# Latent pages turned by transfers and VectorE in a hybrid decoder step

## What is computed

```python
def _decompress(c_kv, w_ukv, g_kn):
    kv = jnp.einsum('btc,chd->bthd', c_kv, w_ukv)
    return _rmsnorm(kv[..., :NOPE], g_kn), kv[..., NOPE:]

def _attn_partial(qn, qp, kn, kp, v, mask):
    s = (jnp.einsum('bqhd,bkhd->bhqk', qn, kn) + jnp.einsum('bqhr,bkr->bhqk', qp, kp)).astype(jnp.float32) * SCALE
    ...
    m = jnp.max(s, axis=-1)
    e = jnp.exp(s - m[..., None])
    return m, jnp.sum(e, axis=-1), jnp.einsum('bhqk,bkhd->bhqd', e, v.astype(jnp.float32))

def _sample_attention(qn, qp, kn_new, kp_new, v_new, cache_ckv, cache_kpe, layer, page_table, w_ukv, g_kn):
    def step(carry, phys):
        c_blk = cache_ckv[layer, phys]
        kp_blk = cache_kpe[layer, phys]
        kn_blk, v_blk = _decompress(c_blk, w_ukv, g_kn)
        return _merge(carry, _attn_partial(qn, qp, kn_blk, kp_blk, v_blk, None)), None
    carry, _ = lax.scan(step, init, page_table.T)
    ...
```

## Time and profile before

| what | value |
|---|---|
| median of 3 runs | 1372.71 us (1370.44 to 1373.48) |
| profiled execution, its own time | 1373.91 us |
| its span in the trace | 1372.0 us |
| TensorE busy | 1301.0 us (95%) |
| VectorE, ScalarE, GpSimd busy | 707.8, 459.9, 150.8 us |
| mean granted TensorE clock | 0.973 |

### The profile page before, as it was taken

How to read it: one execution, slowest core, us unless ns; L and a number is a source line. 1 busy time by engine, 2 the same in 40 slices (tenths; PEclk the granted TensorE clock), 3 DMA queues, 4 the chain that set the end, 5 groups by cost and what they waited for, 6 DMA issues and landing times. The chain is left out here.

```text
span 1372.0 us, 26075 instructions
## 1 busy us (share of the span) xinstructions
PE 1301.0 (95%) x9543; PEld 750.1 (55%) x9543; DVE 707.8 (52%) x1749; ACT 459.9 (34%) x1108; POOL 150.8 (11%) x182
## 2 busy tenths in 40 slices
PE   5999999699999999999989999999999999989898
PEld 3545677556666666555445445666544444445343
DVE  3001436644665656555737876667666666520321
ACT  3001343233343433332434433434344444310220
POOL 0000314400020201114402230000000000000000
PEclk9999999789999999999999999999999999998999
DMA  5422121101111111131141113221334221101000
GB/s 206 155 74 54 32 62 32 52 19 37 37 37 37 37 37 37 37 71 36 40 129 41 40 39 113 97 90 43 86 112 116 68 69 53 49 0 35 16 16 35
DMA packets 82995, 81.49 MB, mean 59 GB/s; under 512 B 18946, under 2 KB 76611, under 8 KB 82868
## 3 DMA queue, kind: packets, MB, share of 16 engines
q1 hardware_dynamic: 80452, 73.87, 18.1%
q10 hardware_dynamic: 2416, 5.96, 1.2%
HBM read 75.72 MB, written 4.07 MB: 58 GB/s over the span
## 5 line engine op out<-in xcount | busy, mean ns | idle before, releaser
L500 PE MATMUL PS<-wk,c_T 128*128 128x512 f32 x1024 | 500.8, 612 | 0.0
L627 DVE TENSOR_REDUCE ssq<-sq__69 128x8 f32<-128x512 f32 x256 | 175.4, 685 | 221.1 <-ACT sq__69 L554 218.7
L500 PEld LDWEIGHTS PS<-wk,c_T 128*128 128x128 f32 x1024 | 176.3, 192 | 163.0 <-issue 145.7
L554 ACT ACTIVATE sq__69<-PS 128x512 f32<-128x512 f32 x256 | 152.8, 597 | 320.5 <-PE PS L500 320.2
L455 PE MATMUL PS<-cst,c_ring 128*128 128x128 f32 x512 | 83.0, 287 | 24.7 <-DVE c_ring L663 10.1
L1470 PE MATMUL PS<-xnT,w_ring 128*128 128x276 f32 x416 | 104.7, 409 | 0.0
L455 PEld LDWEIGHTS PS<-cst,c_ring 128*128 128x128 f32 x512 | 60.4, 147 | 69.7 <-issue 45.0
L1304 PE MATMUL PS<-w_ring,xnT 128*128 128x424 f32 x256 | 95.3, 530 | 2.1 <-DMA w_ring<-in_w_in 2.1
L1470 PEld LDWEIGHTS PS<-xnT,w_ring 128*128 128x128 f32 x416 | 79.9, 195 | 21.9 <-issue 4.1
L1304 PEld LDWEIGHTS PS<-w_ring,xnT 128*128 128x128 f32 x256 | 48.5, 193 | 46.8 <-issue 44.3
L2655 PE MATMUL PS<-w_g,nT 128*128 128x512 f32 x128 | 56.0, 594 | 0.0
(11 more groups left out here) (534 smaller groups left out, 1873.3 us busy)
## 6 DMA issues: line engine op xcount, KB each, us to landing
c_ring<-in_cache_ckv SPq DMA_DIRECT2D x256, 128.0 KB, 2.8
w_ring<-in_w_in SPq DMA_DIRECT2D x4, 1696.0 KB, 14.4
w_ring<-in_w_in SPq DMA_DIRECT2D x9, 512.0 KB, 5.0
r_ring<-in_cache_kpe SPq DMA_DIRECT2D x256, 16.0 KB, 1.8
w_o<-in_w_out SPq DMA_DIRECT2D x8, 512.0 KB, 3.7
w_g<-in_w_ple_gate SPq DMA_DIRECT2D x8, 512.0 KB, 3.6
xn<-in_x_prompt SPq DMA_DIRECT2D x4, 512.0 KB, 7.0
w_ring<-in_w_in SPq DMA_DIRECT2D x2, 1024.0 KB, 5.8
```

The source lines that it names most:

```text
L500: mm = pe.matmul(PS[:, NORM[v % 2], :], c_T[:, u % 2, k, t * P:(t + 1) * P], wk[:, k], start=(k == 0), stop=(k == 1))
L554: nc.scalar.activation(sq_[:, v % 2, :], PS[:, NORM[v % 2], :], ACT.Square).then_inc(no_sb, 1)
L627: dve.tensor_reduce(ssq[:, u % 2, t * H:(t + 1) * H], sq_[:, v % 2, :].rearrange("p (h c) -> p h c", h=H), AX.X, ALU.add).then_inc(red_sb, 1)
```

## The change

The latents are no longer turned on TensorE. `latent_blocks(u)` has ScalarE's queue issue four transfers inside SBUF, each of which puts 64 columns of the four pages on 32 partitions (`c_blocks`, one buffer), in pieces of 64 numbers. VectorE's `turned_c(u, t)` then transposes blocks of 32x32 and writes a page of `c_T`, four instructions a step; `c_T` has one buffer instead of two. The rows of `c_T` thereby stand in another order, and `wk` is loaded in that order by eight transfers instead of being copied from `wukv`. `dots(u)` moves from the last slot to slot 1, beside `values`; `turn_r` moves from slot 2 to slot 0; the copy of `dots_s` moves from VectorE to ScalarE. `c_ring` has five slots, `r_ring` three. In the rows block the first weights are loaded before the second x tile, and several small steps of VectorE, ScalarE, GpSimd and TensorE change places. The blocks for chunks, sequences and latents become one, without the two barriers; the sequences get one more page slot and the last stretch one less. The causal mask of the attention is added by VectorE in PSUM. The output stage keeps its order with some tiles at other addresses.

```diff
-RING = 4
+RING = 5
+R_RING = 3
...
-SEQ_SLOTS = 23
+SEQ_SLOTS = 24
...
-        sc = place("sc", [P, P])
         ew_q = place("ew_q", [P, P])
         ew = place("ew", [P, GT * QH])
         ms = place("ms", [P, 4])
         ring_at = place.at
-        c_T = place("c_T", [P, 2, 2, GT * P])
+        c_ring = place("c_ring", [P, RING, GT, KVL + 1])
+        blocks_at = place.at
+        c_blocks = place("c_blocks", [P, GT, GT, KVL // 4])
+        c_T = place("c_T", [P, 2, GT * P])
+        rope_at = place.at
         r_T = place("r_T", [P, P])
-        r_ring = place("r_ring", [P, RING, GT * ROPE])
+        r_ring = place("r_ring", [P, R_RING, GT * ROPE])
         w_ring_at = t1_at + 4 * (NT * D + KD * TEXT)
-        assert place.at <= w_ring_at
-        pages_at = place.at = w_ring_at
-        c_ring = place("c_ring", [P, RING, GT, KVL + 1])
...
+        def latent_blocks(eng, u):
+            eng.wait_ge(c_in[u % RING], 16 * GT * (u // RING + 1))
+            if u >= 1:
+                eng.wait_ge(ct_sb, u * GT)
+            for g in range(4):
+                eng.dma_start(c_blocks[32 * g:32 * g + 32].rearrange("p x t c -> p (x t c)"),
+                              c_ring[:, slot_of[u], :, g * (KVL // 4):(g + 1) * (KVL // 4)]).then_inc(b_in, 16)
...
-            def turn_c(u, k):
-                if k == 0:
-                    pe.wait_ge(c_in[u % RING], 16 * GT * (u // RING + 1))
-                    if u == 1:
-                        pe.wait_ge(k1_sb, 1)
-                    if u >= 2:
-                        pe.wait_ge(rp_sb, u - 1)
-                else:
-                    pe.wait_ge(k0_sb, u + 1)
-                for t in range(GT):
-                    mm = pe.transpose(PS[:, TURN, t * P:(t + 1) * P], c_ring[:, u % RING, t, k * P:(k + 1) * P], ident)
-                mm.then_inc((k0_ps, k1_ps)[k], 1)
...
             def dots(u):
+                pe.wait_ge(ct_sb, u * GT + GT)
...
             def norms(u, t):
                 v = u * GT + t
-                if t == 0:
-                    pe.wait_ge(k1_sb, u + 1)
+                pe.wait_ge(ct_sb, v + 1)
...
-            pe.wait_ge(ring_ready, 1)
-            turn_c(0, 0)
-            turn_c(0, 1)
+            yield
+            yield
             for u, t in slots:
-                ahead = u + 1 < NSTEP
                 if t == 0:
-                    if ahead:
-                        turn_c(u + 1, 0)
+                    turn_r(u)
                     if u >= 2:
                         turn_weights(u - 2)
                 if t == 1:
-                    if ahead:
-                        turn_c(u + 1, 1)
+                    dots(u)
                     if u >= 2:
                         values(u - 2)
-                if t == 2:
-                    turn_r(u)
-                    if u >= 1:
-                        turn_scale(u - 1)
-                if t == 3:
-                    dots(u)
+                if t == 2 and u >= 1:
+                    turn_scale(u - 1)
                 norms(u, t)
                 yield
...
+            def dotted(u):
+                if u >= 1:
+                    act.wait_ge(eq_sb, u)
+                act.wait_ge(rp_ps, u + 1)
+                nc.scalar.copy(dots_s[:].rearrange("p x c -> p (x c)"), PS[:, TURN, P:3 * P]).then_inc(rp_sb, 1)
...
-            turned_c(0)
+            latent_blocks(act, 0)
+            yield
+            yield
             for u, t in slots:
-                ahead = u + 1 < NSTEP
                 if t == 0:
+                    turned_r(u)
                     if u >= 2:
                         turned_weights(u - 2)
                     if u >= 1:
                         roots(u - 1)
-                    square(u, t)
-                if t == 1:
-                    if ahead:
-                        turned_c(u + 1)
-                    square(u, t)
-                if t == 2:
-                    turned_r(u)
-                    square(u, t)
                 if t == 3:
                     if u >= 1:
                         weights(u - 1)
-                    square(u, t)
+                    dotted(u)
+                square(u, t)
+                if t == 1 and u + 1 < NSTEP:
+                    latent_blocks(act, u + 1)
                 yield
...
-            def turned_c(u):
-                dve.wait_ge(k0_ps, u + 1)
-                dve.tensor_copy(c_T[:, u % 2, 0, :], PS[:, TURN, :]).then_inc(k0_sb, 1)
-
-            def dotted(u):
-                dve.wait_ge(rp_ps, u + 1)
-                dve.tensor_copy(dots_s[:].rearrange("p x c -> p (x c)"), PS[:, TURN, P:3 * P]).then_inc(rp_sb, 1)
+            def turned_c(u, t):
+                dve.wait_ge(b_in, 16 * 4 * (u + 1))
+                if u >= 1:
+                    dve.wait_ge(rp_ps, u)
+                    dve.wait_ge(no_ps, (u - 1) * GT + t + 1)
+                dve.transpose(c_T[:].rearrange("p k (t a x) -> p t x k a", t=GT, x=GT)[:, t],
+                              c_blocks[:, :, t, :].rearrange("p x (k c) -> p x k c", k=2)).then_inc(ct_sb, 1)
...
+            yield
+            for t in range(GT):
+                turned_c(0, t)
             dve.memset(c_ring[:, :, :, KVL:KVL + 1], 1.0).then_inc(ring_ready, 1)
-            turned_c(0)
+            yield
             for u, t in slots:
                 ahead = u + 1 < NSTEP
                 if t == 0:
-                    if ahead:
-                        turned_c(u + 1)
                     if u >= 1:
+                        turned_c(u, 3)
                         scales(u - 1)
                 if t == 1 and u >= 2:
                     merge(u - 2)
-                if t == 2 and u >= 1:
-                    score(u - 1)
-                if t == 3:
-                    dotted(u)
+                if t == 2:
+                    if u >= 1:
+                        score(u - 1)
+                    if ahead:
+                        turned_c(u + 1, 0)
+                if t == 3 and ahead:
+                    turned_c(u + 1, 1)
+                    turned_c(u + 1, 2)
                 reduce(u, t)
                 yield
...
-        on_sp = Stream(pages_sp(), lambda slot: min(NSTEP, max(RING, (slot - 2) // GT + RING - 1)))
+        on_sp = Stream(pages_sp(), lambda slot: min(NSTEP, slot // GT + 3))
...
+                tile_in(0)
                 weights(0)
+                for i in range(1, NT - 1):
+                    tile_in(i)
...
+        def seqs_sp(sp):
+            sp.wait_ge(l_ps, NP)
+            sp.wait_ge(rows_kept, 1)
...
+        def seqs_pe(pe):
+            on_pe.go(1)
+            pe.wait_ge(rows_kept, 1)
+            pe.wait_ge(wkv_sb, 1)
+            pe.wait_ge(half_sb, NP)
...
-        recycle()
         place = Region(nc, shifted_at, t1_at)
...
+                pe.wait_ge(so_sb, BS)
...
+            @block.tensor
+            def _(pe):
+                chunk_pe(pe)
+                seqs_pe(pe)
+                lat_pe(pe)
...
-                    pe.matmul(bank(u % 2)[:, 0:w], qT[:, h, i * P:(i + 1) * P], k_T[:, h, 0:w], start=True, stop=False)
-                    pe.matmul(bank(u % 2)[:, w - P:w], ident, con("causal"), start=False, stop=True).then_inc(sc_ps, 1)
+                    pe.matmul(bank(u % 2)[:, 0:w], qT[:, h, i * P:(i + 1) * P], k_T[:, h, 0:w], start=True, stop=True
+                              ).then_inc(sc_ps, 1)
...
                     dve.wait_ge(sc_ps, u + 1)
+                    V(dve.tensor_tensor(bank(u % 2)[:, w - P:w], bank(u % 2)[:, w - P:w], con("causal"), ALU.add))
```

1657 lines of the change are left out of this document (838 added, 819 removed).

## The result

The changed kernel takes **1602.57 us** (median of 4 runs, 1597.86 to 1613.4), the kernel before 1372.12 beside it: a ratio of 1.169 (95% interval 1.163 to 1.175). The forecast was 1364, its range ended at 1420. The sign was left open; the size is far out. The profiled execution took 1602.05 us, its span is 1600.2.

A forecast was written before the change was run, and what follows sets the result against it. TensorE's queue was taken to bound the kernel. The last stretch at +40 us and the rest at -49 gave -9, from the profiled 1373.9 to 1365, less 1.2 to the median: 1364 us; own range 1335 to 1390, full range 1300 to 1420.

The forecast's parts named there:

- its stations: Last stretch: first issue to first turn 4.9 us, first turn to dot products 2.9, dot products to next issue 3.55.
- Landing: Four transfers in a row: last issued after 1.95 us, lands 2.8 later, page loads add 0.15; 4.9 us.
- The upper bound of 6.6: Landing of the four transfers if their 512 KB move at half the state load's 239 GB/s.
- Rival 2: Small pieces at half rate: landing 6.6 us, step 13.2, last stretch 297, total 1400 us; chance 0.17.
- rival 3: Clock falls to 1.2 GHz in every step: step 14.5 us, last stretch 326, total 1426 us; chance 0.10.
- The turn: VectorE's 128x256 transpose, four a step: 0.41 us each, taken from a copy of as many elements.
- The other stages: All outside the last stretch: -49 us, among it chunks -14, sequences -4, latents -4, attention -10.
- Attention: Attention stage: -8.5 us for turns, -12 for masking matmuls, against VectorE's additions and waits; -10 taken (-18 to +3).
- start and rows: Start and RWKV rows: -2.5 us for earlier first weights, -6 for the first page turn's shorter wait; -8.5.
- the first barrier: Before the sequences: TensorE's 4.6 us idle and 1.5 of slow clock go; -6 us.
- the wait on wukv: Before the latents: the barrier's 5.8 us idle becomes a wait on the wukv weights' load; -2.5 us.
- Rival 1: Transfers hidden, TensorE bounds everywhere: last stretch 199 us, total 1299 us; chance 0.12.

The follow-up runs named there:

- the early issue: The changed kernel with ScalarE's four transfers issued one slot earlier, behind square (u,0) instead of (u,1): 1355.7 us, again 1362.94 us (ratio 0.992).
- the best version: The early issue plus two block buffers from page group 26, one transfer issued a slot, contiguous turns, mask back on TensorE: 1319.27 us, ratio 0.959.

## Why the prediction was wrong

The bound before, the loop and its stations were right: one buffer, the issue behind square (u,1), the first turn waiting, TensorE idle before the first norms. The terms of the sum were not. (The stations of the loop, 4.9, 2.9 and 3.55, add up to 11.35 and not 11.45, and the bounds to a range of 1332 to 1397 and not 1335 to 1390; neither slip matters here.)

- **Landing, 4.9 forecast, 8.0 measured.** The step that failed is "the last is issued after 3 x 0.65 = 1.95 and lands 2.8 later", with page loads at 0.15. Alone the four take 6.4: the first lands after 3.2 us and not 2.8, and the others follow at the 1.0 us that each takes on the engines and not at the 0.65 of their issue. Page loads and rope keys cost the other 1.6, since both kinds start at slot (u,1). The upper bound of 6.6 had the half rate, and was right for it; it lacked the contention.
- **Rival 2 and rival 3 were no alternatives.** I gave the half rate 0.17 and the lower clock 0.10 and priced each alone. A long landing makes the pause longer, the pause takes the clock down, and the slower matmuls stand in the loop. With the pause filled the stations are 7.7, 3.2 and 3.6 against my 4.9, 2.9 and 3.55: 2.8 for the landing and 0.3 for slower turns. The lower clock adds 1.1 us between turn and dot products, 0.75 behind them and 0.3 in the landing: 11.35 + 2.8 + 0.3 + 2.15 is 16.6, the measured median. My own two prices added would have been 13.2 + 3 = 16.2. That it comes near is luck: the 13.2 had no contention in it, and the 3 slowed more work than the clock did.
- **The turn, 0.41 forecast, 0.63 measured.** The row I took was right for the elements; the stride of the output, plain in the diff, was left out. Four a step are 0.9 us of VectorE; with the stride gone, 0.5 of it went out of the way from first turn to dot products (3.2 to 2.7 us at full clock).
- **The other stages, -49 forecast, +83 measured** (the table without its last stretch). The failed step is "the loop of 11.5 is shorter than their step of 15.6". The loop isn't a fixed length to be held against a step: it runs through the stage's own work too, and only what stands between issue and first turn can hide the landing. That is one slot on VectorE, about 4 us (3.7 in the median of the chunks; the forecast had 4.2 and was right in this). But the landing is 8.3 there and not 4.9, so VectorE doesn't stand 0.8 us, as I had it: it stands 73.4 us in 16 steps of the chunks, 46.0 in 15 and 25.4 in 7 of the next two stages, and its evictions for the stage stand behind it. And I priced such a stand at about a third of its length, where the chunks, 50 us above their forecast in 17 steps, lost 2.9 us a step to 4.1 us of standing. With the issue a slot earlier VectorE stands 0.3 us a step there and the chunks come to -12, near the forecast of -14. Sequences and latents come to -6 in one profile and to -1 in the other, against -10.5. For the chunks the terms were right as long as the landing is hidden; for the latents that isn't shown.
- **Attention, -10 forecast, +42 measured, +4 with the early issue.** The landing first: VectorE stands for the blocks, the maximum of the scores stands behind it, and TensorE waits for the exponential 34.7 us in seven stands. Then the mask: I wrote that VectorE and TensorE alternate and still counted the matmuls as mostly a gain. With the early issue ScalarE still waits 77.9 us of the attention for VectorE's maximum (64.2 before).
- **Right in size:** start and rows (-12.6 for -8.5), the first barrier (about 5 us for my 6), the wait on wukv in place of the second. Of the turns' 1.0 us of TensorE a step, 0.7 came: in the best version the step is 9.1 us in the median against 9.85 before.
- Rival 1, the hidden transfers, was priced at 1299 and given 0.12. With them hidden it is 1339 with the parts as they were, 1319 with turns and mask mended. I named its condition, the issue a slot earlier, without asking what that slot was worth: 240 us.

## What to carry to other kernels

Where a transfer replaces work and has one buffer, write down the queue of each engine from the issue to the first use: only that stretch hides the landing, whatever the length of a step. Price issue, landing, contention and clock as one chain, for they feed each other; if two of your rivals share a cause, add their prices. And before dropping a slow change, move its issue up a slot: that is one line.

## What the hardware showed

- Transfers from SBUF to SBUF of 128 KB in pieces of 256 B: 8.0 KB a us on an engine against 16.8 with 1 KB pieces; issued four in a row with nothing beside them, the first lands 3.2 us after its issue and the fourth 4.3, some 1.0 us apart. In the changed kernel's last stretch the median is 5.4. The least seen is 2.7 us, in the version that issues one a slot.
- A 32x32-block turn of 128x256 elements on VectorE takes 428 ns with contiguous output and 626 with output in steps of 16 B; a copy of as many elements took 415.
- A pause of 3.9 us on average before each group of norms goes with a granted clock of 0.81 over the stretch; 3.6 us of useless matmuls in that pause bring it to 1.00 and the time from 1602.6 to 1558.5 us.
- ScalarE issues four transfers in 2.7 us, and no square is done meanwhile; with two buffers, one issue in each slot instead of four in one takes the step from 9.9 to 9.5 us.
